# Running sums of stick-breaking attention: one fp32 product split into two products of rounded operands

## The chip, the cores and the metric

The kernel runs on one core of a Trainium2 chip, in one launch. The metric is the device time in microseconds (us). A profile of one execution accompanies the times. In the profile PE is the matrix engine (TensorE) and PEld its weight loads, DVE is VectorE, ACT is ScalarE, POOL is GpSimd, SP is the engine that issues most DMAs; a q behind a name is that engine's instruction queue.

## The reference

The kernel computes a two-layer decoder trunk: 256 tokens, width 1024, fp32. Layer 0 mixes native sparse attention (NSA, eight heads) with stick-breaking attention (eight heads of 64); layer 1 is a gated linear recurrence. Each layer is followed by a mixture of 32 SwiGLU experts. What the change touches is stick-breaking attention, cut here to its core:

```python
z = jnp.einsum('bqhd,bkhd->bhqk', qb, k).astype(jnp.float32) * ATT_SCALE
log_beta = jax.nn.log_sigmoid(z)
log_keep = jnp.where(before, jax.nn.log_sigmoid(-z), 0.0)
later = lax.cumsum(log_keep, axis=3, reverse=True) - log_keep
a = jnp.where(before, jnp.exp(log_beta + later), 0.0)
return jnp.einsum('bhqk,bkhd->bqhd', a.astype(v.dtype), v)
```

`later` is, for each query, the sum of `log_keep` over the keys that come after key k and before the query.

## The kernel before

Every engine runs its own instruction stream, written out by hand; semaphores order them. There is no loop over tiles of the sequence in the stage of interest: all 256 tokens of one head are one step, with keys on the 128 partitions and queries on the free axis. Keys 0 to 127 see queries 0 to 255 and keys 128 to 255 see queries 128 to 255, so a head is a tile of 128 by 384 (256 + 128 columns).

For head `hd` the steps are these, with the engine that does each:

- PE, `sb_z`: the scores z, for two heads (a pair) at a time, into PSUM bank `SB_BANKS[hd]`: products at L1874 and L1878, and at L1882 the mask, a product of rounded fp32 (`fp32r`, one record in the trace for each matmul).
- DVE, `sb_abs`: max(z, 0) into `zt` (L1263), and z - 2 max(z, 0) = -|z| into `ztmp` (L1264).
- ACT, `exp_ln`: exp (L888) and ln(1 + .) (L889) in place in `ztmp`.
- DVE, L1310: `zt` = max(z, 0) + ln(1 + exp(-|z|)), which is -`log_keep`. Call this step the add.
- PE, `sb_e`: three plain fp32 products of triangular or full matrices of -1 (`later_own`, `later_all`) with `zt`, added onto z in PSUM: L1889 (256 columns), L1890 and L1891 (128 columns each). Each plain fp32 matmul is two records in the trace. The result is log_beta + later.
- ACT, L929: `za` = exp of that.
- PE, `sb_pv` for a pair: `za` times V (L1904), into banks 6 and 7.

`ztmp` has two buffers, `zt` and `za` three. That gives the waits across heads: `sb_abs(hd + 2)` waits until `sb_e(hd - 1)` has read `zt`; `za(hd)` waits, from head 3 on, for an earlier `sb_pv`; `za(5)` waits for `sb_pv(1)` and `za(7)` for `sb_pv(2)`.

The orders written out by hand are:

- PE: the last NSA product `nsa_pv(7)` (L1855), then `sb_z(2)`, `sb_e(0)` to `sb_e(3)`, `sb_pv(0)`, `sb_z(3)`, `sb_e(4)`, `sb_e(5)`, `sb_pv(1)`, `sb_e(6)`, `mix_front(0)`, `sb_e(7)`, `sb_pv(2)`, `sb_pv(3)`, `mix_front(1)`, and then the output projection (`mix_tile`). `mix_front` and `mix_tile` are products of rounded operands (L1697, L1699, L1706).
- DVE: for each head the add, then `sb_abs(hd + 2)`; after head 1 the low part of the NSA output (L1299, twice), after head 6 `sb_out(0)` (L1305 and L1299), after head 7 `sb_out(1)`.
- ACT: for each head `exp_ln(hd + 2)`, at head 0 two copies of the NSA output (L924), then `za(hd)`.

The output projection frees ring units of weights and SP then issues the loads of the layer's experts: L456 for gate and up weights, L464 and L476 to L481 for down weights. The first expert products (L2059) free the buffers for the loads that follow.

The two -1 matrices are made on POOL at the start (L641, L642). The flag behind POOL's constants, `READY["later"]`, is awaited by DVE at L1202, ahead of the operation at L1203. POOL then issues the routing weights (L608). The small inputs are loaded on ACT's queue: the compression's under semaphore `cmp_small`, the recurrence's gain `gnorm` (L795) under `rec_small`. PE waits for `cmp_small` ahead of L1775.

Of the kernel before, what the change touches and what calls it, by code (L numbers as in the profile page):

```python
# [5 lines left out]
F32 = mybir.dt.float32  # L6
F32R = mybir.dt.float32r
I32 = mybir.dt.int32
ALU = mybir.AluOpType
ACT = mybir.ActivationFunctionType  # L10
AX = mybir.AxisListType

P = 128
T = 256
# [140 lines left out]
def hybrid_trunk(nc, x, norm_mix, norm_ffn, att_w_in, att_w_out, cmp_pe_k, cmp_w1_k, cmp_w2_k, cmp_pe_v,  # L155
# [3 lines left out]
    with ctx:  # L159
# [11 lines left out]
        s = Signals()  # L171

        SB_BANKS = (4, 5, 0, 1, 2, 3, 4, 5)
# [4 lines left out]
        xg = sb("xg", [P, TT, D])  # L178
# [28 lines left out]
        gnorm = sb("gnorm", [P, RV])[:, :]  # L207
# [5 lines left out]
        def bank(b):  # L213
            return psum[:, b, :]
# [7 lines left out]
        a = Arena(arena_t)  # L222
# [12 lines left out]
        w2 = a(2, DH)  # L235
# [14 lines left out]
        zt = a(3, 384)  # L250
        za = a(3, 384)
        before_query = a(P)
        later_own = a(P)
        att_front = a.at
        a.at = tail
        a.at += 8 * T
        later_all = a(P)
        ident_r_at = a.at
        a.at += P
# [14 lines left out]
        a = Arena(arena_t)  # L274
# [23 lines left out]
        def rounded(name, shape, place, at=0):  # L298

            return nc.alloc_sbuf_tensor_at(name, shape, F32R, offset=address[place] + at)  # L300
# [17 lines left out]
            return ap.rearrange("p k (g d) -> p k g d", g=NSA_G)  # L318

        ident_r = rounded("ident_r", [P, P], "arena", 4 * ident_r_at)  # L320
        before_r = rounded("before_r", [P, P], "arena", 4 * before_r_at)


# [55 lines left out]
        a = Arena(arena_t)  # L379
# [213 lines left out]
        def _(pool):  # L593
            link = Chain(pool, s["pool_chain"])
# [42 lines left out]
            for dst, fill in ((cmask, NEG), (cvis, 0.0)):  # L637
# [3 lines left out]
            link(pool.memset(later_all[:, :], -1.0))  # L641
            link(pool.affine_select(out=later_own[:, :], in_=later_all[:, :], compare_op=ALU.is_ge, fill=0.0,  # L642
                                    base=0, pattern=[[-1, P]], channel_multiplier=1))
            link(pool.memset(cp[:, :, :, :], 0.0))
            link(pool.memset(hv4[:, :, :, :], 0.0))
            link(pool.memset(ones[:, :], 1.0))
# [66 lines left out]
        def _(act):  # L713
            link = Chain(act, s["act_chain"])
# [74 lines left out]
            act.dma_start(gain[:, :], norm_mix[0].partition_broadcast(P)).then_inc(s["gain_first"], 16)  # L789
            for i, pe in enumerate((cmp_pe_k, cmp_pe_v)):  # L790
                act.dma_start(pe_rows[0:LP, i, :], pe[0].rearrange("(j two) d -> j (two d)", two=2))\
                    .then_inc(s["cmp_small"], 16)
            for i, w in enumerate((cmp_w2_k, cmp_w2_v)):
                act.dma_start(w2[:, i, :], w[0]).then_inc(s["cmp_small"], 16)
            act.dma_start(gnorm[:, :], rec_gnorm[0].partition_broadcast(P)).then_inc(s["rec_small"], 16)  # L795
            for t in range(TT):
                norm(t)
            for t in range(TT):
# [86 lines left out]
            def exp_ln(hd):  # L885
                act.wait_ge(s["sb_abs"], hd + 1)
                v = ztmp[:, hd % 2, :]
                link(act.activation(v, v, ACT.Exp))  # L888
                act.activation(v, v, ACT.Ln, bias=1.0).then_inc(s["sb_ln"], 1)  # L889
# [24 lines left out]
                act.activation(probsT[:, u % 2, 0, :], bank(2), ACT.Copy).then_inc(s["nsa_pT_even"], 1)  # L914


            exp_ln(1)
            for hd in range(SB_H):
                if hd + 2 < SB_H:
                    exp_ln(hd + 2)  # L920
                if hd == 0:
                    act.wait_ge(s["nsa_pv"], 8)
                    for g in range(NSA_G):
                        act.activation(mix_hi[:, 2 * g:2 * g + 2, :], bank(6 + g).rearrange("p (a t) -> p a t", a=2),  # L924
                                       ACT.Copy).then_inc(s["oT_high"], 1)
                act.wait_ge(s["sb_e"], hd + 1)
                if hd >= 3:
                    act.wait_ge(s["sb_pv"], (hd - 3) // 2 * 2 + 2)
                act.activation(za[:, hd % 3, :], bank(SB_BANKS[hd])[:, 0:384], ACT.Exp).then_inc(s["sb_a"], 1)  # L929
# [178 lines left out]
        def _(dve):  # L1108
            link = Chain(dve, s["dve_chain"])
# [147 lines left out]
            def sb_abs(hd):  # L1257

                dve.wait_ge(s["sb_z"], hd + 1)
                if hd >= 3:  # L1260
                    dve.wait_ge(s["sb_e"], hd - 2)
                z, r = bank(SB_BANKS[hd])[:, 0:384], zt[:, hd % 3, :]
                link(dve.tensor_scalar(r, z, 0.0, None, ALU.max))  # L1263
                dve.scalar_tensor_tensor(out=ztmp[:, hd % 2, :], in0=r, scalar=-2.0, in1=z,  # L1264
                                         op0=ALU.mult, op1=ALU.add).then_inc(s["sb_abs"], 1)
# [42 lines left out]
            for hd in range(SB_H):  # L1308
                dve.wait_ge(s["sb_ln"], hd + 1)
                dve.tensor_tensor(zt[:, hd % 3, :], zt[:, hd % 3, :], ztmp[:, hd % 2, :], ALU.add)\  # L1310
                    .then_inc(s["sb_t"], 1)
                if hd + 2 < SB_H:
                    sb_abs(hd + 2)
                if hd == 1:
                    for g in range(NSA_G):
                        dve.wait_ge(s["oT_high"], g + 1)
                        dve.wait_ge(s["proj_psum"], 12)
                        out_low(2 * g, 6 + g)
                if hd == 6:
                    sb_out(0)  # L1320
# [330 lines left out]
        def _(pe):  # L1651
# [118 lines left out]
            proj(1)  # L1770
            free_units(1)

            pe.wait_ge(s["cmp_small"], 64)
            for i in range(2):
                last = pe.transpose(bank(5)[:, i * LP:(i + 1) * LP], pe_rows[0:LP, i, :], ident[0:LP, 0:LP])  # L1775
            last.then_inc(s["cmp_product"], 1)
# [10 lines left out]
            for j in range(LP):  # L1787
                for kv in range(2):
                    last = pe.matmul(bank(5)[64 * kv:64 * kv + WINDOWS, 256:384],
                                     kv2[:, kv].rearrange("p g t -> p (g t)")[:, 2 * j:2 * j + NSA_G * T + 1:CMP_STRIDE],  # L1790
                                     w1[:, kv, j, :], start=(j == 0), stop=(j == LP - 1))
# [8 lines left out]
            for g in range(NSA_G):  # L1800
                last = pe.matmul(bank(5)[:, 64 + g * DH:64 + (g + 1) * DH],
                                 hv4[:, g, :, :].rearrange("p a c -> p (a c)"), w2[:, 1, :], start=True, stop=True)
# [8 lines left out]
            for t in range(TT):  # L1811
                for i in range(HPG):
                    c = (t * HPG + i) * NC
                    for g in range(NSA_G):
                        last = pe.matmul(bank(4 + g)[:, c:c + NC], q_of(g * HPG + i, t), kcT[g * DH:(g + 1) * DH, :],
                                         start=True, stop=True)
# [67 lines left out]
                        .then_inc(s["sb_z"], 1)  # L1884

            def sb_e(hd):
                pe.wait_ge(s["sb_t"], hd + 1)
                z, t = bank(SB_BANKS[hd]), zt[:, hd % 3, :]
                pe.matmul(z[:, 0:T], later_own, t[:, 0:T], start=False, stop=True, skip_group_check=True)  # L1889
                pe.matmul(z[:, P:T], later_all, t[:, T:T + P], start=False, stop=True, skip_group_check=True)  # L1890
                pe.matmul(z[:, T:T + P], later_own, t[:, T:T + P], start=False, stop=True, skip_group_check=True)\  # L1891
                    .then_inc(s["sb_e"], 1)

            def sb_pv(pair):
                pe.wait_ge(s["sb_a"], 2 * pair + 2)
# [13 lines left out]
            for u in range(8):  # L1909
                if u + 1 < 8:  # L1910
                    nsa_scores(u + 1)
                if u == 1:

                    pe.wait_ge(s["cmp_pT_done"], 1)
                    for i in range(HPG):
                        for g in range(NSA_G):
                            last = pe.matmul(bank(6 + g)[i % 2 * DH:(i % 2 + 1) * DH, i // 2 * T:(i // 2 + 1) * T],
                                             vc4[i * 32:(i + 1) * 32, g, :], pcT[i * 32:(i + 1) * 32, g, :],
                                             start=(i < 2), stop=True, skip_group_check=True)
# [242 lines left out]

            for t in range(TT):
                transposes(2, t)
            pe.wait_ge(s["rec_small"], 16)
            pe.wait_ge(s["lb_loaded"], 16)
            pe.transpose(bank(7)[:, 0:2 * RH], lb_rows[0:2 * RH, :], ident[0:2 * RH, 0:2 * RH])\
                .then_inc(s["lb_psum"], 1)
# [34 lines left out]
            for b in range(4):  # L2203
                t, half = b // 2, b % 2
# [7 lines left out]
            for b in range(4):  # L2212
                t, half = b // 2, b % 2
# [84 lines left out]
```

## Time and profile before

| | us |
|---|---|
| median of 3 runs | 758.96 (758.23 to 759.29) |
| the profiled execution | 755.92 |
| its span, first to last instruction | 753.9 |

The profiled execution is 3.0 us below the median of the runs, and 2.0 us of it lie outside the span. All instants below count from the start of the span. Busy time of an engine is a sum over instructions; "granted clock" is the share of TensorE's full 2.4 GHz that was granted, so that 0.50 is 1.2 GHz. A row of the trace with "x2" is a merged group of two instructions. The plan of the span: attention with its projections until about 123 us, the stick-breaking heads until 145, the output projection, norm and routing until 189, the experts of layer 0 until 377, then layer 1 in the same manner.

### The profile page before, as it was taken

What the parts mean: (1) busy time and instruction counts of PE and PEld (TensorE: products, weight loads), DVE (VectorE), ACT (ScalarE), POOL (GpSimd) and SP (SyncE); (2) the same over time, 40 slices, a digit from 0 to 9 for tenths busy, and PEclk for the clock granted to TensorE, in tenths of its full rate; (3) what the DMA queues carried; (4) which work ended last, traced back from release to release, by engine and by line L of the source; (5) the groups of instructions that cost most, each with busy time, mean ns of one, the idle gap of its engine ahead of it and who ended that gap; (6) DMA issues with size and microseconds to landing.
All of it is one profiled execution on the core that took longest, in us unless ns stands there. A gap on an engine that the chain in (4) does not pass through costs nothing.

```text
span 753.9 us, 11975 instructions
## 1 busy us (share of the span) xinstructions
PE 634.8 (84%) x4946; PEld 440.2 (58%) x4946; DVE 314.1 (42%) x536; ACT 225.2 (30%) x494; POOL 35.6 (5%) x62
## 2 busy tenths in 40 slices
PE   6998897999998675865989999999999986595775
PEld 6987786798444322413269999989954441331321
DVE  5455777446132201202275796753542211201204
ACT  5535554431121100100157675552211110110103
POOL 5100000000001100000000001060000000000000
PEclk9999999999999987978899999999999998988978
DMA  8976236469999999999997645429989999999993
GB/s 316 266 258 246 108 113 242 178 263 378 371 420 409 407 422 421 419 422 422 411 387 263 225 157 207 170 82 421 393 323 423 418 422 420 421 422 420 422 416 153
DMA packets 59506, 246.10 MB, mean 326 GB/s; under 512 B 4496, under 2 KB 8832, under 8 KB 38208
## 3 DMA queue, kind: packets, MB, share of 16 engines
q1 hardware_dynamic: 57824, 242.33, 81.7%
q0 software_dynamic: 992, 2.40, 1.0%
q8 instruction: 35, 0.57, 0.3%
q10 hardware_dynamic: 640, 0.67, 0.3%
q14 instruction: 15, 0.12, 0.0%
HBM read 244.34 MB, written 1.05 MB: 325 GB/s over the span
## 4 chain that ended last, share of the span: by engine, by line
PE 51%; DMA 32%; SPq 6%; DVE 5%; ACT 3%; issue 2%; DVEq 0%; ACTq 0%
DMA ring<-in_moe_w_down 30%; PE psum L1697 8%; PE psum L2114 7%; PE psum L2059 6%; PE psum L1706 5%; PE psum L1699 5%; PE psum L1708 3%; PE psum L1701 3%; SPq L488 3%; PE psum L2052 2%; DMA ring<-in_att_w_in 2%; SPq L464 2%; PE psum L1669 1%; PE psum L2043 1%; ACT w_hi L750 1%
## 5 line engine op out<-in xcount | busy, mean ns | idle before, releaser
L2059 PE MATMUL psum<-arena,xT 128*32 128x512 f32 x512 | 66.2, 676 | 38.1 <-DMA arena<-in_moe_w_up 38.1
L1438 DVE TENSOR_TENSOR arena<-psum,arena 128x256 f32<-128x256 f32 x16 | 6.8, 425 | 217.2 <-ACT arena L952 217.2
L2059 PE MATMUL psum<-ring,xT 128*32 128x512 f32 x512 | 64.5, 661 | 32.0 <-DMA ring<-in_moe_w_up 32.0
L2114 PE MATMUL psum<-ring,arena 128*32 128x512 f32 x464 | 61.9, 627 | 12.6 <-DMA ring<-in_moe_w_down 12.5
L948 ACT ACTIVATE arena<-psum 128x256 f32<-128x256 f32 x16 | 6.1, 383 | 204.6 <-PE psum L2059 204.6
L2059 PEld LDWEIGHTS psum<-arena,xT 128*32 128x32 f32 x512 | 18.1, 122 | 81.6 <-issue 46.2
L1697 PE MATMUL psum<-x_hi,w_hi 128*128 128x256 f32 x248 | 61.7, 287 | 2.1 <-DVE x_hi L1128 1.2
L750 ACT ACTIVATE w_hi<-ring 128x1024 fp32r<-128x1024 f32 x48 | 48.8, 1051 | 45.8 <-PE psum L1708 19.2
L2052 PE MATMUL psum<-arena,xg 128*128 128x128 f32 x512 | 60.3, 275 | 0.7 <-DVE arena L1425 0.7
L368 DVE TENSOR_TENSOR w_lo<-ring,w_hi 128x1024 fp32r<-128x1024 f32 x44 | 52.3, 1221 | 18.4 <-ACT w_hi L750 18.4
L2059 PEld LDWEIGHTS psum<-ring,xT 128*32 128x32 f32 x512 | 16.7, 120 | 73.9 <-issue 40.6
L2052 PEld LDWEIGHTS psum<-arena,xg 128*128 128x128 f32 x512 | 58.6, 192 | 0.9 <-DVE arena L1425 0.9
L2043 PE MATMUL psum<-xT,arena 128*128 128x512 f32 x128 | 57.7, 594 | 0.0
L1697 PEld LDWEIGHTS psum<-x_hi,w_hi 128*128 128x128 f32 x248 | 47.3, 191 | 3.8 <-issue 1.6
L1421 DVE TENSOR_TENSOR h<-psum,h 128x512 f32<-128x512 f32 x64 | 44.2, 690 | 9.3 <-PE psum L2043 8.2
L1701 PE MATMUL psum<-x_hi,w_lo 128*128 128x256 f32 x192 | 47.0, 283 | 0.0
L2114 PEld LDWEIGHTS psum<-ring,arena 128*32 128x32 f32 x464 | 15.8, 114 | 51.5 <-issue 35.5
L1697 PE MATMUL psum<-w_hi,x_hi 128*128 128x256 f32 x160 | 39.7, 286 | 0.9 <-issue 0.8
L1699 PE MATMUL psum<-w_lo,x_hi 128*128 128x256 f32 x160 | 39.2, 283 | 0.0
L2043 PEld LDWEIGHTS psum<-xT,arena 128*128 128x128 f32 x128 | 23.1, 190 | 24.6 <-issue 24.6
L1701 PEld LDWEIGHTS psum<-x_hi,w_lo 128*128 128x128 f32 x192 | 36.8, 192 | 0.0
L1708 PE MATMUL psum<-x_lo,w_hi 128*128 128x256 f32 x248 | 34.8, 283 | 0.1
(327 smaller groups left out, 1044.8 us busy)
## 6 DMA issues: line engine op xcount, KB each, us to landing
ring<-in_moe_w_down SPq DMA_DIRECT2D x58, 1024.0 KB, 20.5
ring<-in_moe_w_gate SPq DMA_DIRECT2D x32, 1024.0 KB, 17.6
ring<-in_moe_w_up SPq DMA_DIRECT2D x32, 1024.0 KB, 19.6
arena<-in_moe_w_gate SPq DMA_DIRECT2D x32, 1024.0 KB, 22.4
arena<-in_moe_w_up SPq DMA_DIRECT2D x32, 1024.0 KB, 24.7
ring<-in_rec_w_in SPq DMA_DIRECT2D x16, 1024.0 KB, 13.9
ring<-in_att_w_in SPq DMA_DIRECT2D x8, 1024.0 KB, 11.5
ring<-in_att_w_out SPq DMA_DIRECT2D x4, 1024.0 KB, 13.8
```

The lines of the kernel that those rows point to most:

```text
L368: eng.tensor_tensor(quarter_lo(base, r), quarter(base, r), quarter_hi(r).bitcast(F32), ALU.subtract)\
L750: act.activation(quarter_hi(r), quarter(base, r), ACT.Copy).then_inc(s["w_high"], 1)
L1421: dve.tensor_tensor(v, bank(b), v, ALU.add).then_inc(done, 1)
L1697: pe.matmul(dst, a_hi(k), b_hi(k), start=(k == 0), stop=False)
L1699: pe.matmul(dst, a_hi(k), b_lo(k), start=False, stop=False)
L1701: pe.matmul(dst, a_lo(k), b_hi(k), start=False, stop=False)
L1706: last = pe.matmul(dst, a_lo(k), b_hi(k), start=False, stop=(k == KD - 1))
L1708: last = pe.matmul(dst, a_hi(k), b_lo(k), start=False, stop=(k == KD - 1))
L2043: pe.matmul(bank(b), shareT[:, t, :], y_rows[:, half * 512:(half + 1) * 512], start=True, stop=True).then_inc(s[f"combined{l}"], 1)
L2052: last = pe.matmul(bank(k // 4)[:, k % 4 * P:(k % 4 + 1) * P], xg_parts[:, t, k, :], slots[:, t].rearrange("p e c -> p (e c)"), start=(t = ...
L2059: return pe.matmul(bank(3)[e * CAP:(e + 1) * CAP, :].rearrange("p (w f) -> p w f", w=2), gatheredT[:, k, e * CAP:(e + 1) * CAP], w, start= ...
L2114: last = pe.matmul(bank(5 + c)[e * CAP:(e + 1) * CAP, :], hidT[:, j, e * CAP:(e + 1) * CAP], down_part(l, kind, e, j)[:, c * 512:(c + 1) * ...
```

## The change

The running sums are computed from two rounded halves in place of one exact operand. ACT copies `zt` to `t_hi`, rounded to `fp32r` (`sum_high`). DVE computes `t_lo = zt - t_hi`, also `fp32r`. `sb_e` does its three products twice, once for each half, with `fp32r` operands throughout: six matmuls of one record each in place of three of two. `t_hi` and `t_lo` have two buffers each. Two more casts on POOL make rounded copies of the -1 matrices, in place. The semaphores `cmp_small` and `rec_small` become one, `small_loaded`.

```diff
@@ names
+        later_own_r = rounded("later_own_r", [P, P], "arena", 4 * later_own_at)
+        later_all_r = rounded("later_all_r", [P, P], "arena", 4 * later_all_at)
+        t_hi = rounded("t_hi", [P, 2, 384], "xg")
+        t_lo = rounded("t_lo", [P, 2, 384], "xg", 4 * 2 * 384)
@@ POOL, behind L642
+            link(pool.tensor_copy(later_own_r[:, :], later_own))
+            link(pool.tensor_copy(later_all_r[:, :], later_all))
@@ ACT, L792 to L795
-                    .then_inc(s["cmp_small"], 16)
+                    .then_inc(s["small_loaded"], 16)
...
-            act.dma_start(gnorm[:, :], rec_gnorm[0].partition_broadcast(P)).then_inc(s["rec_small"], 16)
+            act.dma_start(gnorm[:, :], rec_gnorm[0].partition_broadcast(P)).then_inc(s["small_loaded"], 16)
@@ ACT, L917
+            def sum_high(hd):
+                act.wait_ge(s["sb_t"], 2 * hd + 1)
+                if hd >= 2:
+                    act.wait_ge(s["sb_e"], hd - 1)
+                act.activation(t_hi[:, hd % 2, :], zt[:, hd % 3, :], ACT.Copy).then_inc(s["sb_high"], 1)
             exp_ln(1)
             for hd in range(SB_H):
+                sum_high(hd)
                 if hd + 2 < SB_H:
                     exp_ln(hd + 2)
@@ DVE, L1313
                 if hd + 2 < SB_H:
                     sb_abs(hd + 2)
+                dve.wait_ge(s["sb_high"], hd + 1)
+                dve.tensor_tensor(t_lo[:, hd % 2, :], zt[:, hd % 3, :], t_hi[:, hd % 2, :].bitcast(F32), ALU.subtract)\
+                    .then_inc(s["sb_t"], 1)
@@ PE, L1773 and L2165
-            pe.wait_ge(s["cmp_small"], 64)
+            pe.wait_ge(s["small_loaded"], 80)
@@ PE, L1886
             def sb_e(hd):
-                pe.wait_ge(s["sb_t"], hd + 1)
-                z, t = bank(SB_BANKS[hd]), zt[:, hd % 3, :]
-                pe.matmul(z[:, 0:T], later_own, t[:, 0:T], start=False, stop=True, skip_group_check=True)
-                pe.matmul(z[:, P:T], later_all, t[:, T:T + P], start=False, stop=True, skip_group_check=True)
-                pe.matmul(z[:, T:T + P], later_own, t[:, T:T + P], start=False, stop=True, skip_group_check=True)\
-                    .then_inc(s["sb_e"], 1)
+                z = bank(SB_BANKS[hd])
+                for t, ready in ((t_hi, (s["sb_high"], hd + 1)), (t_lo, (s["sb_t"], 2 * hd + 2))):
+                    pe.wait_ge(*ready)
+                    t = t[:, hd % 2, :]
+                    pe.matmul(z[:, 0:T], later_own_r[:, :], t[:, 0:T], start=False, stop=True, skip_group_check=True)
+                    pe.matmul(z[:, P:T], later_all_r[:, :], t[:, T:T + P], start=False, stop=True,
+                              skip_group_check=True)
+                    last = pe.matmul(z[:, T:T + P], later_own_r[:, :], t[:, T:T + P], start=False, stop=True,
+                                     skip_group_check=True)
+                last.then_inc(s["sb_e"], 1)
```

## Rows read from the trace of the kernel before

**Rows 1.** The stages: range, length, busy us (x instructions) by engine, PEclk, DMA share, GB/s.

```profile
123.10:145.30 22.20, 17.98 (x129) 14.18 (x129) 12.75 (x25) 12.60 (x27) 0.00 (x0) 0.92 0.47 190
...
145.30:167.40 22.10, 21.83 (x182) 21.33 (x180) 9.74 (x14) 7.37 (x22) 0.00 (x0) 1.00 0.75 287
167.40:189.30 21.90, 20.69 (x192) 18.25 (x196) 14.20 (x49) 4.22 (x16) 0.61 (x2) 1.00 0.84 336
189.30:377.50 188.20, 146.12 (x1049) 63.61 (x1041) 39.62 (x71) 23.34 (x54) 5.12 (x8) 0.89 1.01 414
377.50:540.00 162.50, 157.26 (x1286) 149.48 (x1287) 106.14 (x144) 89.16 (x171) 16.01 (x15) 1.00 0.67 249
```

**Rows 2.** SP's queue between 145 and 190 us, in order of time.

```profile
145.36 0.33 SPq L456 DMA_DIRECT2D arena<-in_moe_w_gate  x1
...
189.29 0.33 SPq L456 DMA_DIRECT2D ring<-in_moe_w_gate  x1
```

**Rows 3.** The chain that ended last, 123 to 175 us: start, us, what.

```profile
125.87 0.43 PE psum L1889 x2
126.31 0.22 PE psum L1890 x2
126.53 0.24 PE psum L1891 x2
...
127.93 1.28 DVE mix_lo L1299 x2
...
132.48 0.43 PE psum L1890 x2
...
151.81 0.94 PE psum L1706 x8
...
169.54 0.87 PE psum L1661 x8
```

**Rows 4.** Groups between 119 and 147 us: busy us, mean ns of one, idle before.

```profile
L1264 DVE SCALAR_TENSOR_TENSOR arena<-arena,psum 128x384 f32<-128x384 f32 x8 | 4.4, 554 | 0.3
...
L1310 DVE TENSOR_TENSOR arena<-arena 128x384 f32<-128x384 f32 x8 | 4.4, 550 | 0.0
...
L888 ACT ACTIVATE arena<-arena 128x384 f32<-128x384 f32 x8 | 4.2, 522 | 8.6 <-DVE arena L1264 8.5
```

**Rows 5.** Instructions of the stage in order of time: start, us, engine, line, tile.

```profile
125.71 0.60 PE L1889 MATMUL psum<-arena 128*128 128x256 f32 x2
...
126.79 0.49 ACT L929 ACTIVATE arena<-psum 128x384 f32<-128x384 f32 x1
...
133.26 1.43 PE L1904 MATMUL psum<-arena 128*64 128x256 f32 x8
...
136.02 0.56 DVE L1263 TENSOR_SCALAR arena<-psum 128x384 f32<-128x384 f32 x1 [3.29 <-PE psum L1882]
...
138.76 0.87 PE L1904 MATMUL psum<-arena 128*64 128x256 f32 x8
...
140.46 0.36 PE L1697 MATMUL psum<-mix_w_hi,mix_hi 128*128 128x256 f32 x1
...
142.93 0.87 PE L1904 MATMUL psum<-arena 128*64 128x256 f32 x8
...
145.25 0.39 PE L1697 MATMUL psum<-mix_w_hi,mix_hi 128*128 128x256 f32 x1
```

**Rows 6.** Two short stretches, columns as in the first group.

```profile
127.60:131.00 3.40, 1.17 (x7) 0.90 (x6) 3.37 (x7) 1.66 (x4) 0.00 (x0) 1.00 1.00 417
...
132.00:133.00 1.00, 1.00 (x6) 0.91 (x4) 0.72 (x2) 0.90 (x3) 0.00 (x0) 0.50 0.99 418
```

**Rows 7.** A cast on POOL, and POOL's first DMA, in order of time.

```profile
8.03 1.19 POOL L656 CAST before_r<-arena 128x128 fp32r<-128x128 f32 x1
...
10.86 0.99 POOL L608 DMA_DIRECT2D w_route<-in_moe_w_grp  x1
```

**Rows 8.** DVE's first use of POOL's constants, from the chain that ended last.

```profile
49.88 0.23 DVE arena L1203
```

More of the change, by code:

```diff
@@ L252, in hybrid_trunk @@
         before_query = a(P)
+        later_own_at = a.at
         later_own = a(P)
@@ L256, in hybrid_trunk @@
         a.at += 8 * T
+        later_all_at = a.at
         later_all = a(P)
@@ L791, in _ @@
                 act.dma_start(pe_rows[0:LP, i, :], pe[0].rearrange("(j two) d -> j (two d)", two=2))\
-                    .then_inc(s["cmp_small"], 16)
+                    .then_inc(s["small_loaded"], 16)
             for i, w in enumerate((cmp_w2_k, cmp_w2_v)):
-                act.dma_start(w2[:, i, :], w[0]).then_inc(s["cmp_small"], 16)
-            act.dma_start(gnorm[:, :], rec_gnorm[0].partition_broadcast(P)).then_inc(s["rec_small"], 16)
+                act.dma_start(w2[:, i, :], w[0]).then_inc(s["small_loaded"], 16)
+            act.dma_start(gnorm[:, :], rec_gnorm[0].partition_broadcast(P)).then_inc(s["small_loaded"], 16)
             for t in range(TT):
@@ L2164, in _ @@
                 transposes(2, t)
-            pe.wait_ge(s["rec_small"], 16)
+            pe.wait_ge(s["small_loaded"], 80)
             pe.wait_ge(s["lb_loaded"], 16)
```

## Prediction, made before the kernel was changed

> **What bounds the kernel now.** I read the times by stage first [rows 1]. The reader should see three regimes. From 123.1 to 145.3 us, where the changed code runs, no engine is full: PE is busy 17.98 us of 22.20, DVE 12.75, ACT 12.60, and DMA has a share of 0.47. From 145.3 to 189.3 PE is nearly full (21.83 of 22.10, then 20.69 of 21.90). From 189.3 to 377.5 the DMA share is 1.01: the experts' weights set the time. Then PE again (157.26 of 162.50).
>
> The next question is whether a shift of the stick-breaking stage reaches the end. SP's queue answers it [rows 2]: the load at 145.36 waits for the last `sb_pv`, and the one at 189.29, with which the full DMA stretch begins, waits for the first expert product, which stands behind all of the attention on PE. Before it DMA has gaps (0.75, 0.84 [rows 1]), so there is no backlog to absorb a delay. I carry a shift of the instant at which the output projection begins, 145.25 [rows 5], one to one to the end, in either direction.
>
> Last I read the stage itself, by chain, groups and order of time [rows 3 to 5]. It is a relay: PE makes z, DVE two passes, ACT two, DVE the add, PE `sb_e`, ACT the exponential. What matters is the length of the relay and what each step stands behind on its engine, more than any busy share.
>
> **The products.** Now: L1889 takes 0.43 us, L1890 0.22, L1891 0.24 at full clock [rows 3], so 0.89 a head. New: six matmuls of one record. With 256 moving columns a rounded product takes 0.94/8 = 0.118 (L1706); eight transposes of 128 columns, each with a weight load, take 0.87, so 0.109 each (L1661) [rows 3]. No row shows a rounded product with 128 moving columns. By the moving columns alone it would be half of 0.118, 0.059; at the rate of the plain product, 0.22. I take 0.109, the row nearest in shape. A half is then 0.118 + 2 x 0.109 = 0.34, and both 0.67: 0.22 less a head, 1.7 over eight heads as PE work. The ends are 0.24 for a half (0.1 less) and 0.56 (0.22 more).
>
> The Trainium skill, page "TensorE: Matmul & The Clock Gate", section "LDWEIGHTS (loading the stationary operand)", gives a weight load as the columns of the stationary operand over 1.2 GHz. By that rule 128 columns take about 0.107 and a product of 128 moving columns is bound by its load; the 0.109 agrees. With 0.059 in its place the products would cost 0.2 less a head, with the rule as with the row they do not.
>
> **The two new passes.** ACT's copy of 384 columns: L888 has the shape and 0.522 [rows 4]; I take 0.52. DVE's subtraction: L1310 has the shape and both sources in SBUF, 0.55 [rows 4]; I take that. A handover between engines I set at 0.05, and an end of `sb_e` some 0.12 behind its last issue. So from the end of a subtraction to the end of `sb_e`, as its reader sees it, 0.05 + 0.34 + 0.12 + 0.05 = 0.56.
>
> **Where they stand, head by head, at full clock.** DVE does add(hd), the two passes of `sb_abs(hd+2)`, then the new subtraction lo(hd). ACT does the copy hi(hd) ahead of `exp_ln(hd+2)`, but behind the exponential `za(hd-1)`.
>
> Head 0 is covered: PE reaches `sb_e(0)` only at about 125.6, behind `sb_z(2)` (its first product is the 125.71 of [rows 5]), and lo(0) is done by 125.3. Head 1 is not. Before, `sb_e(1)` followed `sb_e(0)` without a gap. Now hi(1) stands on ACT behind za(0), which ends at 126.79 + 0.49 = 127.28 [rows 5]. So hi(1) ends at 127.8 and lo(1) at 128.4. Behind it on DVE stand the two L1299 (1.28 [rows 3]), to 129.7, then add(2) and `sb_abs(4)` to 131.4, and lo(2) to 131.95. `sb_abs(5)` needs `sb_e(2)`, 0.56 later (add(3) fits in between), so 132.5 to 133.6; lo(3) ends at 134.15. The low half of `sb_e(3)` lets `sb_pv(0)` start at about 134.7, against 133.26 [rows 5]: **+1.4**.
>
> `sb_z(3)` is behind `sb_pv(0)` on PE, and `sb_abs(6)` waits for it. `sb_pv(0)` is 0.87 at full clock (the 138.76 row [rows 5]) and `sb_z(3)` with its latency 1.3, so `sb_abs(6)` starts at 136.9 against 136.02 [rows 5]. Then DVE passes back to back: 1.1, lo(4) 0.55, add(5) 0.55, `sb_abs(7)` 1.1, lo(5) 0.55, to 140.8 with overlaps of some 0.05. `sb_pv(1)` starts at 141.2 against 138.76 [rows 5]: **+2.45**.
>
> `za(5)` waits for `sb_pv(1)`, so to about 142.2. What was harmless is now ahead of hi(6): 0.49 for za(5), 0.52 for hi(6), 0.55 for lo(6), 0.34 and handovers for the low half, and only then `mix_front(0)`, at 144.2 against 140.46 [rows 5]: **+3.75**. On DVE `sb_out(0)` (1.4) stands ahead of add(7); then 0.55, 0.52, 0.55 for add, hi and lo of head 7, to 146.9, and `sb_pv(2)` at 147.3 against 142.93 [rows 5]: **+4.35**. The rest (za(7), `sb_pv(3)`, `mix_front(1)`) runs as before, with 0.1 for gaps: the projection begins at 149.7 against 145.25: **+4.45**.
>
> **The clock.** In the stretch 127.6 to 131.0 PE was busy 1.17 us of 3.40, and after it the granted clock is 0.50, the lower level, 1.2 GHz [rows 6]. There L1890 takes 0.43 in place of 0.22 [rows 3] and `sb_pv(0)` 1.43 in place of 0.87 [rows 5]. The walk above is at full clock throughout. In it PE works from 126.3 to 134.6 only six halves, 2 us of 8, so the clock will fall again, and it can fall again after 137 and 142. What lies on the path then doubles: the low halves (0.34 each), `sb_pv(0)` (0.87) and `sb_z(3)` (about 1.2). With two low halves and most of the other two, 0.7 + 1.3, I take **+2.0**. Its ends are 0 and about 5 (low throughout to 150, `mix_front` included).
>
> The Trainium skill, same page, section "HAM oscillation — how this bites in real kernels", says that a matrix engine that waits between short bursts drops to the lower level again and again. The fall behind the idle stretch agrees; how often it recurs no row here shows.
>
> **What costs nothing.** Two casts on POOL, 1.19 each (L656), shift POOL's first DMA from 10.86 to about 13.3 [rows 7]; DVE first needs the constants at 49.88 [rows 8], and the routing weights only behind the projection, near 167. With that cover gone it would be 2.4. The merged semaphore makes PE wait in layer 0 also for `gnorm`, a small load issued on the same queue right behind the others, well ahead of PE's second projection: 0; no bound above that beyond a fraction of a microsecond.
>
> **Sum.** 4.45 + 2.0 = 6.4. Against its own time, 755.92 + 6.4 = 762.3; the median of the runs lies 3.0 higher, so 758.96 + 6.4 = **765.4**.
>
> **Rivals.**
> - *PE is the bound and the passes are covered* (faster). DVE and ACT are idle 9.5 us each of 22.2 [rows 1], and eight passes of 0.55 or 0.52 would fit. Then the 0.22 a head counts: 1.7, so 757.3. It decides if hi and lo of a head are ready whenever PE gets to it. Against: by the walk PE is free for `sb_e(1)` at 126.3 and its low half is ready at 128.4, and so on for each head from there. Chance 0.06.
> - *Gain and loss cancel.* Only the tail (heads 6 and 7) is exposed, +1.9, less 1.7: 759.2. Chance 0.06.
> - *The clock stays low* through most of the stage and into the projection: 4.45 + 4 to 5, so 768. For it: the thin work of PE. Against: `sb_pv(0)`, `sb_z(3)` and `sb_e(4)` make over 3 us of dense work, after which it could rise. Chance 0.16.
> - *The shift is swallowed* before 189: 760.5 if 5 of 6.4 were. Nothing in [rows 1] offers the room. Chance 0.04.
> - My forecast: 0.68, with its own range 762.5 to 768.
>
> **Range and chances.** The lower end takes 4.45 without any loss to the clock, less 0.8 for cheap narrow products (8 x 0.1), and leaves room for part of the last rival: 761.8. The upper end is the low-clock case with narrow products at the plain rate on the path (some five halves, 1.1): 769.5. The measurement tells about 0.2% (1.5 us) from no change. Faster 0.06, same 0.06, slower 0.88.
>
> **What would show it.** Right: `sb_pv(0)`, `sb_pv(1)`, `mix_front(0)`, `sb_pv(2)` and `mix_front(1)` start later by 1.4, 2.45, 3.75, 4.35 and 4.45, plus what the clock adds; PE idle ahead of both halves, put down to ACT and DVE; a granted clock of 0.50 in more of the stage; all later stages of the same length. Wrong: L1889 and its neighbours start back to back with the high half as they did; or a narrow rounded product that takes 0.06 or 0.22; or a stage from 189.3 that is shorter by what the first one lost. The forecast fails most easily in the clock's term.

## The result, and the profile of the changed kernel

The changed kernel takes 769.16 us in the median of 5 runs (766.08 to 769.30) against 758.96 (755.74 to 759.29): a ratio of 1.0125, 95% interval 1.0105 to 1.0145, slower by some 10 us. The forecast was 765.4 with a range of 761.8 to 769.5: the direction and the mechanism hold, the size was too small by 3.8.

The profiled execution took 769.3 us, with a span of 767.6. First the stages, as in [rows 1], with the columns as there:

```profile
127.20:158.60 31.40, 23.10 (x129) 18.11 (x129) 16.76 (x33) 16.43 (x35) 0.00 (x0) 0.67 0.34 134
158.60:180.70 22.10, 21.84 (x182) 21.34 (x180) 9.73 (x14) 7.38 (x22) 0.00 (x0) 1.00 0.75 286
180.70:202.60 21.90, 20.69 (x192) 18.25 (x196) 14.20 (x49) 4.22 (x16) 0.61 (x2) 1.00 0.86 336
202.60:391.00 188.40, 143.50 (x1052) 63.37 (x1044) 39.59 (x71) 23.37 (x54) 5.14 (x8) 0.90 1.01 414
391.00:553.50 162.50, 157.27 (x1286) 149.50 (x1287) 106.14 (x144) 89.19 (x171) 16.02 (x15) 1.00 0.68 248
```

Only the stick-breaking stage changed its length: 31.4 us against 22.2 [rows 1]. The four that follow are 22.1, 21.9, 188.4 and 162.5, as before to within 0.2. So the shift was carried one to one, also through the stretch in which DMA sets the time. SP's queue shows the carrying, against 145.36 and 189.29 [rows 2]; both moved by 13.3:

```profile
158.67 0.33 SPq L463 DMA_DIRECT2D arena<-in_moe_w_gate  x1
...
202.59 0.33 SPq L463 DMA_DIRECT2D ring<-in_moe_w_gate  x1
```

Of these 13.3 us, 4.1 arose ahead of the changed steps: the first add of the stage is at 127.23 here and at 123.14 in the profile before. That part is a difference between executions. In the first 120 us both kernels run the same work on PE and differ in the clock. The same five microseconds, in the kernel before (first row) and in the changed kernel (second fence):

```profile
55.00:60.00 5.00, 5.00 (x45) 4.87 (x43) 1.02 (x3) 0.41 (x1) 0.00 (x0) 1.00 1.05 392
```

```profile
55.00:60.00 5.00, 5.00 (x28) 4.96 (x27) 1.69 (x6) 0.41 (x1) 0.00 (x0) 0.50 1.05 399
```

45 matmuls against 28 in the same time, at a granted clock of 1.00 and of 0.50. Profiles of kernels that are alike up to there differ by over 2 us in the same way: the first add lies at 127.23 in the changed kernel and at 124.80 in e5 below. The rest of the change is not the reason: in e9, which has only that rest (the casts on POOL and the one semaphore), the first add lies at 124.06. That is why all readings below count from the first add of the stage.

Counted so, the stage of the changed kernel takes 31.33 us to the first product of `mix_front(1)`, before 22.11: 9.2 more, against 10.2 between the medians.

**The instants of the walk.** The instructions that answer to those of [rows 5], in order of time (L1928 is `sb_pv`, L1280 the first pass of `sb_abs`):

```profile
139.08 1.55 PE L1928 MATMUL psum<-arena 128*64 128x256 f32 x8
...
142.88 0.56 DVE L1280 TENSOR_SCALAR arena<-psum 128x384 f32<-128x384 f32 x1 [4.22 <-PE psum L1902]
...
147.72 1.55 PE L1928 MATMUL psum<-arena 128*64 128x256 f32 x8
...
151.67 0.52 PE L1717 MATMUL psum<-mix_w_hi,mix_hi 128*128 128x256 f32 x1
...
155.64 1.46 PE L1928 MATMUL psum<-arena 128*64 128x256 f32 x8
...
158.56 0.39 PE L1717 MATMUL psum<-mix_w_hi,mix_hi 128*128 128x256 f32 x1
```

| us from the first add | before | changed | shift | predicted at full clock |
|---|---|---|---|---|
| `sb_pv(0)` | 10.12 | 11.85 | +1.7 | +1.4 |
| `sb_pv(1)` | 15.62 | 20.49 | +4.9 | +2.45 |
| `mix_front(0)` | 17.32 | 24.44 | +7.1 | +3.75 |
| `sb_pv(2)` | 19.79 | 28.41 | +8.6 | +4.35 |
| `mix_front(1)` | 22.11 | 31.33 | +9.2 | +4.45 |

The first three `sb_pv` take 1.55, 1.55 and 1.46 us; before, only `sb_pv(0)` was slow (1.43) and the others took 0.87. The reason is in the clock, three stretches of the changed kernel with the columns of the first fence:

```profile
133.00:143.20 10.20, 7.50 (x33) 5.76 (x33) 5.31 (x11) 4.87 (x10) 0.00 (x0) 0.50 0.71 295
143.20:146.60 3.40, 1.35 (x9) 0.97 (x7) 3.07 (x7) 2.15 (x5) 0.00 (x0) 1.00 0.00 0
146.60:156.70 10.10, 8.81 (x42) 7.36 (x43) 3.58 (x7) 2.76 (x6) 0.00 (x0) 0.50 0.00 1
```

Between 133.0 and 156.7 the granted clock is 0.50 (1.2 GHz) for 20.3 us of 23.7. It rises once in between, at 143.2, at the end of the dense stretch of `sb_pv(0)`, `sb_z(3)` and the high half of head 4 (137.4 to 143.5), so that this work itself ran at the lower clock. PE is then busy for 1.35 us of 3.40, and the clock falls again. It was back at 1.00 only at 156.7, in `sb_pv(2)`. Before, the stage had a mean of 0.92 [rows 1], now 0.67.

**Who waits for whom** in the stage of the changed kernel, longest first (us in total, times, longest):

```profile
ACT arena L946 <- PE psum L1928: 7.8, 3, 4.0
...
PE psum L1911 <- ACT t_hi L931: 5.9, 5, 1.7
...
DVE t_lo L1332 <- ACT t_hi L931: 3.6, 2, 3.0
```

PE waits 5.9 us for ACT's copy (L931) ahead of high halves, and 1.3 us for the subtraction (L1332) ahead of low ones. In the kernel before it waited in these places for the add alone, 3.2 us in all:

```profile
PE psum L1889 <- DVE arena L1310: 3.2, 3, 2.1
```

The copy itself waits for nothing but the add (0.9 us in all), so the two buffers of `t_hi` and `t_lo` are enough. The first row above is `za(5)` behind `sb_pv(1)` and its like: what ACT does after it, the copy for head 6 first of all, waits along, and DVE's subtraction for head 6 waits 3.0 us for it.

**The new steps by themselves**, groups of the stage (busy us, mean ns, idle before):

```profile
L1332 DVE TENSOR_TENSOR t_lo<-arena,t_hi 128x384 fp32r<-128x384 f32 x8 | 4.4, 552 | 3.6 <-ACT t_hi L931 3.6
...
L931 ACT ACTIVATE t_hi<-arena 128x384 fp32r<-128x384 f32 x8 | 4.1, 518 | 0.9 <-DVE arena L1327 0.9
```

The passes cost what the prediction took, 0.55 and 0.52. The products of head 0, at full clock, in order of time:

```profile
129.80 0.28 PE L1911 MATMUL psum<-t_hi,later_own_r 128*128 128x256 f32 x1
129.80 0.19 PEld L1912 LDWEIGHTS psum<-t_hi,later_all_r 128*128 128x128 f32 x1
...
129.92 0.22 PE L1912 MATMUL psum<-t_hi,later_all_r 128*128 128x128 f32 x1
129.92 0.19 PEld L1914 LDWEIGHTS psum<-t_hi,later_own_r 128*128 128x128 f32 x1
129.98 0.28 PE L1914 MATMUL psum<-t_hi,later_own_r 128*128 128x128 f32 x1
...
130.09 0.33 PE L1911 MATMUL psum<-t_lo,later_own_r 128*128 128x256 f32 x1
```

From the product with 256 columns to the next start it is 0.12, and from there only 0.06. That is not what a narrow product costs, for the next half starts 0.11 behind: the two narrow ones take 0.17 together. The weight loads show the pace. Six products on end, one head of the experiment e11 below, at full clock (the last row is the load of a spare matmul behind them):

```profile
129.56 0.19 PEld L1909 LDWEIGHTS psum<-zt_r,later_own_r 128*128 128x128 f32 x1
129.67 0.19 PEld L1910 LDWEIGHTS psum<-zt_r,later_all_r 128*128 128x128 f32 x1
129.80 0.19 PEld L1912 LDWEIGHTS psum<-zt_r,later_own_r 128*128 128x128 f32 x1
129.90 0.19 PEld L1909 LDWEIGHTS psum<-zt_r,zero_r 128*128 128x128 f32 x1
130.02 0.19 PEld L1910 LDWEIGHTS psum<-zt_r,zero_r 128*128 128x128 f32 x1
130.14 0.19 PEld L1912 LDWEIGHTS psum<-zt_r,zero_r 128*128 128x128 f32 x1
130.25 0.30 PEld L1680 LDWEIGHTS psum<-ident 128*128 128x128 f32 x2
```

The loads start 0.10 to 0.13 apart, whatever the width of the product. Six of them take 0.69, 0.34 to 0.35 for a half, and that is what the prediction took (0.34 and 0.67).

### The profile page after: what moved, and what is told of

Its sections match the earlier page's. It is cut to its first block, busy times and chain, and to the rows that moved or that the text cites. A ratio compares the mean times of both kernels' runs of the same rounds, so it can differ in the third digit from the quotient of the medians.

```text
span 767.6 us, 11999 instructions
## 1 busy us (share of the span) xinstructions
PE 642.6 (84%) x4946; PEld 449.0 (58%) x4946; DVE 318.1 (41%) x544; ACT 229.2 (30%) x502; POOL 35.9 (5%) x64
## 4 chain that ended last, share of the span: by engine, by line
PE 52%; DMA 31%; DVE 6%; SPq 5%; ACT 3%; issue 2%; DVEq 0%; ACTq 0%
DMA ring<-in_moe_w_down 30%; PE psum L1717 9%; PE psum L2138 6%; PE psum L2083 5%; PE psum L1726 5%; PE psum L1719 5%; PE psum L1728 4%; PE psum L1721 3%; SPq L495 3%; PE psum L2076 2%; SPq L471 2%; DMA ring<-in_att_w_in 2%; PE psum L1689 1%; PE psum L2067 1%; PE psum L1875 1%
## 5 line engine op out<-in xcount | busy, mean ns | idle before, releaser
L2138 PE MATMUL psum<-ring,arena 128*32 128x512 f32 x464 | 59.9, 608 | 13.5 <-DMA ring<-in_moe_w_down 13.5
L1717 PE MATMUL psum<-x_hi,w_hi 128*128 128x256 f32 x248 | 63.5, 293 | 1.5 <-DVE x_hi L1145 1.2
L2076 PE MATMUL psum<-arena,xg 128*128 128x128 f32 x512 | 60.3, 275 | 0.7 <-DVE arena L1445 0.7
L2076 PEld LDWEIGHTS psum<-arena,xg 128*128 128x128 f32 x512 | 58.6, 192 | 0.9 <-DVE arena L1445 0.9
```

The lines of the kernel that those rows point to most:

```text
L1717: pe.matmul(dst, a_hi(k), b_hi(k), start=(k == 0), stop=False)
L2076: last = pe.matmul(bank(k // 4)[:, k % 4 * P:(k % 4 + 1) * P], xg_parts[:, t, k, :], slots[:, t].rearrange("p e c -> p (e c)"), start=(t = ...
L2138: last = pe.matmul(bank(5 + c)[e * CAP:(e + 1) * CAP, :], hidT[:, j, e * CAP:(e + 1) * CAP], down_part(l, kind, e, j)[:, c * 512:(c + 1) * ...
```

## The experiments

The experiments ran in three sets: e1 to e4; e5, e7, e8 and e9; e6, e10 and e11. In each set all kernels ran on the same chip, beside runs of the kernel before (its medians 757.84, 757.80 and 758.24, with 17, 29 and 26 runs); a time is compared with the kernel before of its own set, the changed kernel's with the 758.96 above. "Stage" is the time from the first add to `mix_front(1)` in one profile.

| | stage, us | time, us | less the kernel before | ratio, 95% interval |
|---|---|---|---|---|
| before | 22.11 | | | |
| changed | 31.33 | 769.16 | +10.2 | 1.0105 to 1.0145 |
| e2 passes only | 35.41 | 770.54 | +12.7 | 1.0157 to 1.0206 |
| e3 products only | 22.96 | 759.31 | +1.5 | 1.0007 to 1.0037 |
| e5 changed, spare matmuls | 26.23 | 761.26 | +3.5 | 1.0024 to 1.0059 |
| e6 before, spare matmuls | 20.63 | 756.83 | -1.4 | 0.9968 to 0.9995 |
| e7 before, spare matmuls twice | 20.61 | 759.08 | +1.3 | 1.0002 to 1.0033 |
| e8 copy first | 29.17 | 765.72 | +7.9 | 1.0067 to 1.0118 |
| e9 rest only | 22.19 | 758.55 | +0.7 | 0.9989 to 1.0017 |
| e10 copy first, spare matmuls | 25.17 | 761.36 | +3.1 | 1.0030 to 1.0058 |
| e11 products only, spare matmuls | 19.42 | 755.85 | -2.4 | 0.9958 to 0.9986 |

The differences of the stages and of the medians agree within 1.0 us in all but e7, whose second group of spare matmuls lies ahead of the stage.

**e1 and e4: spare matmuls, first form.** Spare products of `ident` with itself were put on PE where it waits, into columns 384 to 511 of the head's own bank, which the head does not use:

```diff
+            def fill(n, b):
+                for _ in range(n):
+                    pe.matmul(bank(b)[:, 384:512], ident[:, :], ident[:, :], start=True, stop=True,
+                              skip_group_check=True)
...
             def sb_e(hd):
+                fill(FILL_AT.get(hd, 0), SB_BANKS[hd])
```

For e1, on the changed kernel:

> The changed kernel, with spare 128x128 fp32 matmuls (0.21 us each at full clock, into unused columns of the head's own PSUM bank) put on PE in the gaps ahead of the halves of the running sums. Theory (the relay costs 4.2 to 4.5 us at full clock and the lower clock the other 5): granted clock near 1.00 through the stick-breaking stage, the stage 4 to 5 us shorter than in the changed kernel, time 764 to 765. Rival (the passes on ACT and DVE alone make the stage longer, the clock is only a companion): no gain, or the spare matmuls come on top, 769 to 771.

For e4, on the kernel before:

> The kernel before with spare 128x128 fp32 matmuls ahead of the sums of heads 2, 3 and 5, where PE waits. Theory: the granted clock stays at 1.00 between 127 and 138 us, and the 1.7 us that the lower clock costs there come back: 757.3. Rival: PE waits for DVE there anyway, so the spare work buys nothing: 759.

They took 3148.17 and 1711.92 us, and tell nothing of the whole time. Both left the course of the kernel behind the stage: the first expert products (L2059 before, L2076 here) are 512 matmuls in the changed kernel, 3072 in e1 and 1536 in e4, so the experts' loops ran more passes. The likely way there is that the sum started in unused columns changed the running sums in the other columns of the bank, and that with other values in the attention output the routing sent more tokens to single experts; the same spare matmuls with `start=False` (e5, e6) leave the loops as they were. The heads of the two pages, e1's and then e4's, have the number of instructions (11999 in the changed kernel, 12187 in e5):

```profile
span 3146.8 us, 40151 instructions
```

```profile
span 1708.1 us, 23215 instructions
```

Their stage is still good to read: the granted clock is 1.00 in all of it, and it takes 26.23 and 20.64 us.

**e5: spare matmuls on the changed kernel.** As e1, with `start=False`:

```diff
-                    pe.matmul(bank(b)[:, 384:512], ident[:, :], ident[:, :], start=True, stop=True,
+                    pe.matmul(bank(b)[:, 384:512], ident[:, :], ident[:, :], start=False, stop=True,
...
+            FILL_AT = {(1, True): 7, (1, False): 1, (2, True): 8, (2, False): 3, (3, True): 5, (3, False): 1,
+                       (4, False): 6, (5, True): 5, (5, False): 1, (6, True): 5, (6, False): 1,
+                       (7, True): 3, (7, False): 1}
...
                 for t, ready in ((t_hi, (s["sb_high"], hd + 1)), (t_lo, (s["sb_t"], 2 * hd + 2))):
+                    fill(FILL_AT.get((hd, t is t_hi), 0), SB_BANKS[hd])
                     pe.wait_ge(*ready)
```

> The same as e1, with spare matmuls that add to the unused columns (start=False) in place of starting a new sum there, so that the sums in the rest of the bank keep their state. Theory: granted clock 1.00 through the stage, 26.2 us from the first add to the projection in place of 31.3, time 763.5 to 765. Rival (the clock is only a companion of the passes): 768 to 771.

Its whole stage, with the columns as above:

```profile
124.80:151.00 26.20, 25.22 (x222) 22.67 (x222) 16.73 (x33) 16.35 (x33) 0.00 (x0) 1.00 0.41 162
```

The granted clock is 1.00 where it was 0.67, and the stage is 5.1 us shorter (26.23 against 31.33), although PE has 47 spare matmuls more to do. The time fell to 761.26, below the range expected. DVE is busy 16.73 us and ACT 16.35, as without the spare work: the passes are the same, only PE's clock differs, and all `sb_pv` take 0.87. So the rival falls. The clock cost 5.1 of the changed kernel's stage, or a little more, for with PE busy 25.22 us of 26.20 a spare matmul may here and there stand ahead of a half that is ready.

**e6: spare matmuls on the kernel before**, 8, 1 and 4 of them ahead of heads 2, 3 and 5:

> The kernel before with spare matmuls in the stick-breaking stage alone (8, 1 and 4 of them ahead of the sums of heads 2, 3 and 5, adding to unused columns). Theory: the stage, from the first add to the projection, takes 20.6 us in place of 22.1 and the time is 1.5 below the kernel before, 756.3. Rival (what the stage gains is lost in the clock further on): 757.8.

```profile
124.40:145.10 20.70, 19.20 (x155) 16.07 (x155) 12.77 (x25) 12.53 (x27) 0.00 (x0) 1.00 0.51 203
```

As expected: the stage takes 20.63 us, the time is 756.83, 1.4 less than the kernel before in its set, a ratio of 0.9981 (0.9968 to 0.9995). In the kernel before the clock cost 1.5 us of the stage. This version is faster than both kernels, than the one before by a small margin.

**e2: the passes alone.** The copy and the subtraction stay, the products are the plain ones of before, waiting for the subtraction:

```diff
             def sb_e(hd):
+                pe.wait_ge(s["sb_t"], 2 * hd + 2)
+                z, t = bank(SB_BANKS[hd]), zt[:, hd % 3, :]
+                pe.matmul(z[:, 0:T], later_own, t[:, 0:T], start=False, stop=True, skip_group_check=True)
...
```

> The changed kernel with its copy on ACT and its subtraction on DVE, but the sums as the three plain fp32 products of the kernel before, which wait for the subtraction and don't read its result; no casts on POOL. Theory (the two passes in the relay are the loss, the rounded products a small gain): at full clock 0.53 us more per head than the changed kernel on the path, for seven heads some 3.5, but PE is busier in the stage; so 769 to 773. Rival (the products in six pieces are the loss): near the kernel before, 759 to 761.

770.54 us, with a stage of 35.41, 4.1 longer than the changed kernel's. The passes are the loss. Here the whole sum stands behind the subtraction, in the changed kernel only the low half does; that split and the cheaper products together are worth the 4.1.

**e3: the products alone.** The add writes its result rounded, six rounded products read it, three of them with zeros:

```diff
+                z, t = bank(SB_BANKS[hd]), zt_r[:, hd % 3, :]
+                pe.wait_ge(s["sb_t"], hd + 1)
+                for own, every in ((later_own_r, later_all_r), (zero_r, zero_r)):
...
-                dve.tensor_tensor(zt[:, hd % 3, :], zt[:, hd % 3, :], ztmp[:, hd % 2, :], ALU.add)\
+                dve.tensor_tensor(zt_r[:, hd % 3, :], zt[:, hd % 3, :], ztmp[:, hd % 2, :], ALU.add)\
```

> The kernel before with the add writing its result rounded, and the sums as six rounded products that all read it, the second three with a matrix of zeros, so that the low part of the values is left out of the sums; no copy, no subtraction. Theory: a head's products take about 0.5 us in place of 0.87 and stand nowhere behind a new pass, so the stage is 0 to 2 us shorter at full clock; with less work on PE the clock may fall for longer and give 1 to 2 back: 757 to 760. Rival (six pieces are the loss): 763 or more.

759.31 us, 1.5 more than the kernel before: even with no new pass the cheaper products did not pay. They are cheaper by less than the expectation has it: some 0.69 a head (the loads of e11, above) against 0.89 [rows 3], not 0.5. The stage of e3:

```profile
124.70:147.70 23.00, 18.74 (x129) 15.24 (x129) 12.81 (x25) 12.55 (x27) 0.00 (x0) 0.78 0.45 183
```

The granted clock has a mean of 0.78, before 0.92 [rows 1]. Behind the stage the work is that of the kernel before (11978 instructions against 11975), so the missing low part does not disturb the comparison.

**e11: the products alone, with spare matmuls** (9, 2 and 5 of them, ahead of heads 2, 3 and 5; the low part is left out as in e3):

```diff
                 z, t = bank(SB_BANKS[hd]), zt_r[:, hd % 3, :]
+                fill({2: 9, 3: 2, 5: 5}.get(hd, 0), SB_BANKS[hd])
```

> The rounded products alone (low part left out of the sums, second three products with zeros, no copy, no subtraction), with spare matmuls ahead of the sums of heads 2, 3 and 5. Theory (cheaper products gain on the path, and without spare work lose it to the clock): the stage takes 19.3 to 20 us against 20.6 for the plain products with spare matmuls, time 755 to 756.3. Rival (the products don't lie on the path): 20.6 us, 756.5.

As expected, with 755.85 us. The stage takes 19.42 us, 1.2 less than e6 and 3.5 less than e3; its granted clock is 1.00 throughout. Six rounded products a head are worth 1.2 us on the path at full clock (a head's six take 0.2 less than its three plain ones), and without spare work the stage loses 3.5 us to the clock, where the plain products lose 1.5.

**e8: the copy ahead of the exponential**, in ACT's order:

```diff
             for hd in range(SB_H):
-                sum_high(hd)
                 if hd + 2 < SB_H:
                     exp_ln(hd + 2)
...
+                if hd + 1 < SB_H:
+                    sum_high(hd + 1)
                 act.wait_ge(s["sb_e"], hd + 1)
```

> The changed kernel, with the copy of the next head's values ahead of the exponential of this one in ACT's order, so that the high halves of heads 1, 6 and 7 no longer stand behind an exponential. Theory (the places in ACT's order cost part of the relay): 1.5 to 2 us less than the changed kernel at full clock, so 766 to 768. Rival (only DVE's order matters, ACT's is covered): 768.5 to 769.5.

765.72 us, just below the range expected, and 29.17 in the stage: 2.2 less than the changed kernel. ACT around head 6, in order of time (L931 is the copy, L948 the exponential):

```profile
146.40 0.51 ACT L931 ACTIVATE t_hi<-arena 128x384 fp32r<-128x384 f32 x1
148.39 0.49 ACT L948 ACTIVATE arena<-psum 128x384 f32<-128x384 f32 x1 [1.49 <-PE psum L1930]
```

The copy for head 6 is done 1.5 us before `za(5)` may start. `sb_pv(1)` is at 20.48 us as in the changed kernel (20.49), `sb_pv(2)` at 26.85 against 28.41: all of the gain lies in the last two heads, where the prediction's walk had put `za(5)` in the way. At head 1, which the expectation also named, nothing is gained. Of the 2.2 us 0.6 is the clock: `sb_pv(2)` takes 0.87 here and 1.46 in the changed kernel.

**e10: both mendings** on the changed kernel:

> The changed kernel with both mendings: ACT's copy ahead of the exponential, and the spare matmuls. Theory (the two add up): the stage takes 24.6 us, the time is 1.6 below the one with spare matmuls alone, 759.5 to 760.5, still above the kernel before. Rival (they mend the same loss): 761 to 762.

A miss: the stage takes 25.17 us, 1.1 less than e5 in place of the 1.6 expected, and the time, 761.36, lies in the rival's range. Against the kernel before of its own set it is +3.1, e5 +3.5, and these two can't be told apart. So the copy's place costs 1.1 of the stage at full clock and 2.2 at the changed kernel's clock; part of e8's gain and of e5's is the same loss. The two passes in the relay stay, and with them 4.5 us over e6.

**e7: spare matmuls in two places** on the kernel before, those of e6 and twelve ahead of L1799:

```diff
+            keep_clock(12, 7)
             pe.wait_ge(s["cmp_step"], CMP_STEP["h"])
```

> The kernel before with spare matmuls in the stick-breaking stage (ahead of the sums of heads 2, 3 and 5, adding to unused columns) and also twelve ahead of the compressed keys' products at L1799, where PE waits some 3 us and the clock falls in some executions. Theory: 1.5 us from the stage, and up to 2 more from the executions in which the clock fell near 55 us: 754.5 to 756.5, with less spread. Rival (lost clock elsewhere is hidden): 757.5 to 758.

A miss: 759.08. The stage took 20.61, so its gain was there, but its first add was at 127.24, and the granted clock between 50 and 60 us still fell to a mean of 0.83. That PE has time at L1799 was wrongly read: it is busy with a projection until then, and the twelve spare matmuls, from 50.22 to the next product at 53.09, came on top with 2.9 us.

**e9: the rest alone.** The casts on POOL and the merged semaphore, without copy, subtraction and rounded products:

> The kernel before with only the rest of the change: the two casts on POOL and the one semaphore for the small loads; the products stay plain fp32, no copy and no subtraction. Theory: no difference, 757.5 to 759. Rival (the later end of POOL's constants, or the wait for the last small load, shifts the projections): 760 or more.

758.55 us, ratio 0.9989 to 1.0017: no difference that can be told, and none above 1.3 us. In the changed kernel POOL's two new casts take 0.29 and 0.30 us, and its first DMA is at 11.21 against 10.86 [rows 7], 0.35 later where the prediction had 2.4.

## Why the prediction was right, and where it was short

**The relay, right.** The walk gave 4.45 us at full clock over the stage of before. It set the new steps at full clock against the kernel before as it was, with its own 1.5 us of lower clock. The changed kernel at full clock (e5) takes 26.23 us against 22.11: 4.1. Its instants agree too: in e5 `sb_pv(0)`, `sb_pv(1)`, `mix_front(0)` and `sb_pv(2)` are at 11.23, 17.93, 20.84 and 23.91 us, that is +1.1, +2.3, +3.5 and +4.1, against +1.4, +2.45, +3.75 and +4.35. The difference of 0.3 is there from the first instant on. It comes mostly from DVE, whose passes the walk mostly laid end to end, 0.55 each, where e5 shows most of them starting 0.47 behind one another: the subtraction for head 3 ends 10.7 us behind the first add in e5, by the walk 11.0. A part was given back on the way: `sb_abs(5)` starts 0.80 behind the subtraction for head 2, where the walk had 0.56.

**The products, right.** The prediction took 0.34 for a half and 0.67 for both; the loads of e11 give 0.34 to 0.35 and 0.69. A start 0.06 behind another, which it had named as a sign of being wrong, does occur within a half, but the half as a whole is no shorter for it. The rule of the Trainium skill (page "TensorE: Matmul & The Clock Gate", section "LDWEIGHTS (loading the stationary operand)"), by which 128 columns take about 0.107, agrees with the loads, 0.10 to 0.13 apart. On the path too the term holds: in e5 `sb_pv(0)` starts 0.54 behind the end of the subtraction for head 3, where the walk had 0.55.

**The clock, the term that failed.** The prediction took +2.0 with ends 0 and 5. It measured 5.1 (31.33 less 26.23), the upper end, and that is the rival "the clock stays low", which had a chance of 0.16 and gave 768. The step that failed is the argument against it: that `sb_pv(0)`, `sb_z(3)` and `sb_e(4)` make over 3 us of dense work after which the clock could rise. It did rise, but at 143.2, when that work was nearly done, and it fell again at 146.6, after the next heads had left PE idle. The sum of +2.0 held two low halves and most of `sb_pv(0)` and `sb_z(3)`, and nothing behind them. Measured (changed kernel less e5), the clock had cost 2.6 us by `sb_pv(1)`, and 2.5 more behind it. The sum by measured terms is 4.1 + 5.1 = 9.2, against 6.4. The 10.2 between the medians has an interval of 8.0 to 11.0 us, so the other 1.0 is not resolved. That 769.16 still lies under the upper end of 769.5 is in part luck: that end holds 1.1 for narrow products at the plain rate, which did not come.

**The rivals.** "PE is the bound" falls with e5 and e2: at full clock the changed kernel's stage is 5.6 us longer than e6's, and with the passes and the old products the kernel loses 12.7. "Gain and loss cancel" falls with the table of instants: the loss begins at head 1 and grows at every pair. "The shift is swallowed" falls with the stages, equal to within 0.2 us. What was to cost nothing cost nothing that can be told (e9).

**Where the whole 9.2 us come from**, in stage times at full clock and at the granted one:

| | at full clock | at the granted clock | the clock's share |
|---|---|---|---|
| plain products (e6, before) | 20.63 | 22.11 | 1.5 |
| rounded products (e11, e3) | 19.42 | 22.96 | 3.5 |
| rounded products and the two passes (e5, changed) | 26.23 | 31.33 | 5.1 |

The product's saving is 1.2 us, the passes cost 6.8 at full clock (1.1 of it ACT's order, e10), and the clock's share grew with each step: less work on PE in the second row, longer waits in the third. Each stage time is one profile. e3 and e11 have their second three products behind the same add, so that 6.8 holds the wait between the halves as well.

**Open.** What decides in which executions the clock falls between 50 and 65 us, which moves the first add by over 2 us, was not found; e7 was one try. A low part made without the hop over ACT, by DVE alone, wasn't tried.

## What to carry to other kernels

In a relay of short steps over several engines, price an edit by where each new step stands in its engine's order, and what late wait stands ahead of it; the busy shares of 57% and less here promised a cover that did not exist. And price TensorE's clock together with the edit: work taken off PE in a stage where it already waits can be more than given back by the clock (1.2 us saved, 2.0 us more lost, in e11 and e3 against e6 and the kernel before), and here a few spare matmuls in the gaps were worth more than the saving. They have to go where PE waits: in e7 twelve of them cost 2.9 us. If spare matmuls are added to a bank in use, they must not start a sum.

## What the runs showed of the hardware that had not been expected

- Spare matmuls that start a new sum in columns 384 to 511, which no one reads, changed what came out of the stage; with `start=False` they did not (e1 and e4, against e5 and e6, which differ in that flag alone: 40151 and 23215 instructions against 12187 and 12027). The Trainium skill gives the reason, page "PSUM — Partial Sum Buffer", section "The four PSUM rules": the first matmul of a group clears the flags that decide between adding and overwriting for a whole region, beyond the columns that it writes. The two pairs of runs agree.
- Rounded matmuls with 128 moving columns can start 0.06 us apart at full clock, but a run of them among wider ones is no faster than its weight loads of 128 columns, 0.10 to 0.13 apart (e11).
- The cast of L656 on POOL took 1.19 us in the kernel before and 0.29 in the changed one (9.40, the same cast), where two casts more stand ahead of it. In e3, with three more ahead, it took 1.16 again; why was not found.
- Spare work made PE's real work faster: 222 matmul records in 26.2 us against 129 in 31.4, for the same sums and products of the stage.
